# A hybrid encoder layer on one core: a third weight buffer, another step order in the linear attention, another split of the expert work over the engines, and expert products scattered by pair

## The reference

```
h = rmsnorm(x, norm_mix);  proj = h @ w_in
ya = (dilated window attention, 3 groups of 4 heads, merged by log-sum-exp) @ w_proj_a
o_f, o_b = gla_chunked(q, k, v, logg_f), flipped gla_chunked(...)      # 4 heads, chunks of 64
yb = (rmsnorm(o_f + o_b, gla_norm) * silu(og)) @ w_proj_b
x = x + (sigmoid(ma) * ya + sigmoid(mb) * yb) @ w_out
hm = rmsnorm(x, norm_moe)
# hier_moe: top-1 of 4 groups, top-2 of its 8 experts -> gate, zero elsewhere
for e in range(N_EXPERTS):                                             # 32 experts, inner width 256
    a = jax.nn.silu(h @ w_eg[e]) * (h @ w_eu[e])
    out = out + gate[:, e:e + 1] * (a @ w_ed[e])
x = x + out;  y = rmsnorm(x, norm_final)
```

## Time and profile before

| | us |
|---|---|
| median of three timed runs | 1405.68 |
| lowest and highest of them | 1402.28, 1409.32 |
| profiled execution, its own time | 1400.52 |
| span of its trace, first to last instruction | 1398.7 |
| expert stage in it, first gate product to last down product | 981.6 to 1359.5 |

### The profile page before, as it was taken

One profiled execution on the slowest core, in us unless ns is written; L12 is line 12 of the kernel. 1 busy time (PEld: TensorE's weight loads), 2 busy tenths in 40 slices (PEclk: granted clock), 3 DMA queues, 4 the chain that ended last, 5 costly groups with the idle time before them and its releaser, 6 DMA issues. The chain is left out here.

```text
span 1398.7 us, 19631 instructions
## 1 busy us (share of the span) xinstructions
PE 1206.4 (86%) x7864; PEld 1112.9 (80%) x7864; DVE 637.6 (46%) x1063; ACT 555.2 (40%) x905; POOL 443.8 (32%) x196
## 2 busy tenths in 40 slices
PE   5989999988989889999999989951888988889870
PEld 3989899787778678999999989951877877878860
DVE  5001312446534354522021041266477787887856
ACT  6223443435435253221122130241466566665622
POOL 2121120221020110221121151243466666666613
PEclk8999999998999999999999999975899999999985
DMA  6520101442130310212122123172599999999927
GB/s 245 177 61 30 31 10 41 119 126 57 35 91 1 91 40 10 77 38 68 61 68 68 60 95 107 40 255 98 177 320 327 304 340 343 349 338 315 337 108 270
DMA packets 158728, 200.39 MB, mean 143 GB/s; under 512 B 11625, under 2 KB 139773, under 8 KB 158654
## 3 DMA queue, kind: packets, MB, share of 16 engines
q1 hardware_dynamic: 151150, 183.41, 40.2%
q0 software_dynamic: 7504, 15.94, 3.3%
HBM read 179.32 MB, written 34.42 MB: 153 GB/s over the span
## 5 line engine op out<-in xcount | busy, mean ns | idle before, releaser
L841 POOL TENSOR_TENSOR w_lo<-raw,w_hi 128x2048 fp32r<-128x2048 f32 (+2 forms) x37 | 152.7, 4126 | 667.8 <-ACT w_hi L979 667.6
L1206 PE MATMUL bank<-hT_hi,w_hi 128*128 128x384 f32 (+1 forms) x656 | 225.6, 344 | 4.3 <-DVE hT_lo L1493 4.3
L1207 PE MATMUL bank<-hT_lo,w_hi 128*128 128x384 f32 (+1 forms) x656 | 222.1, 339 | 0.0
L1208 PE MATMUL bank<-hT_hi,w_lo 128*128 128x384 f32 (+1 forms) x656 | 222.1, 339 | 0.0
L900 POOL TENSOR_TENSOR lo_gate<-raw_gate,hi_gate 128x2048 fp32r<-128x2048 f32 x30 | 138.6, 4619 | 114.3 <-ACT hi_gate L968 114.2
L1753 DVE TENSOR_TENSOR lo_up<-raw_up,hi_up 128x2048 fp32r<-128x2048 f32 x31 | 112.7, 3634 | 51.6 <-ACT hi_up L968 51.6
L1206 PEld LDWEIGHTS bank<-hT_hi,w_hi 128*128 128x128 f32 (+1 forms) x656 | 124.3, 189 | 8.3 <-DVE hT_lo L1493 4.7
L1207 PEld LDWEIGHTS bank<-hT_lo,w_hi 128*128 128x128 f32 (+1 forms) x656 | 124.3, 190 | 0.9
L1208 PEld LDWEIGHTS bank<-hT_hi,w_lo 128*128 128x128 f32 (+1 forms) x656 | 124.0, 189 | 1.0
L1206 PE MATMUL bank<-w_hi,hT_hi 128*128 128x256 f32 x432 | 123.7, 286 | 0.0
L1208 PE MATMUL bank<-w_hi,hT_lo 128*128 128x256 f32 x432 | 123.0, 285 | 0.0
(11 more groups left out here) (289 smaller groups left out, 2908.3 us busy)
## 6 DMA issues: line engine op xcount, KB each, us to landing
raw_gate<-in_w_exp_gate SPq DMA_DIRECT2D x32, 1024.0 KB, 7.5
raw_up<-in_w_exp_up SPq DMA_DIRECT2D x32, 1024.0 KB, 10.5
raw_down<-in_w_exp_down SPq DMA_DIRECT2D x32, 1024.0 KB, 5.6
raw<-in_w_in SPq DMA_DIRECT2D x25, 1024.0 KB, 6.0
y_d<-m_y SPq DMA_DIRECT2D x32, 512.0 KB
y_d<-zeros SPq DMA_DIRECT2D x11, 512.0 KB, 7.3
raw<-in_w_in SPq DMA_DIRECT2D x8, 512.0 KB, 6.2
raw<-in_w_proj_b SPq DMA_DIRECT2D x4, 1024.0 KB, 5.0
```

Source lines behind the costliest of these rows:

```text
L841: pool.tensor_tensor(w_lo[:, g % 2, 0:kb, 0:n], raw[:, g % 2, 0:kb, 0:n], w_hi[:, g % 2, 0:kb, 0:n].bitcast(F32), ALU.subtract).then_inc(w ...
L1206: pe.matmul(out, l_hi, r_hi, start=j == 0, stop=False)
L1207: pe.matmul(out, l_hi, r_lo, start=False, stop=False)
L1208: ins = pe.matmul(out, l_lo, r_hi, start=False, stop=j == n - 1)
```

## The change

The source differs in five places.

1. `raw` and `w_lo` share three buffers, and the subtraction writes over its input. A group's load waits for the last product of the group three before it.
2. The list of steps: `comb` and all `mix` stand together; `decay` is cut into `soft`, `cumul` and `decay`; z and soft of head h+1 stand behind `kot` of head h, cumul in the midst of its states and outputs, and the six products of `vb` h+1 are spread among those. `vb` has two buffers. For the last head, `mb` 0 is spread in their place.
3. The experts: DVE takes over the subtraction for gate, ACT takes over `result`, PE runs gate e+1, aT e, xt e+2, up e+1, down e. POOL is left with index copies and indirect DMAs.
4. `y_d` has 1536 rows, one for each pair; POOL scatters the product rows there with an indirect DMA, in place of SP's stores. Rows of a slot that hold no pair have a number beyond the bound and move nothing. SP then reads `y_pair` in token order with six plain DMAs. The 11 stores of zeros go.
5. Gate, up and router weights are laid out `(p k) n`, eight consecutive rows of the matrix to a partition, with h2 permuted to match.

```diff
-        raw = at("raw", [P, 2, KD, GW], F32, 56)
+        raw = at("raw", [P, RAW, KD, GW], F32, 56)
+        w_lo = at("w_lo", [P, RAW, KD, GW], F32R, 56)
...
+        head = [S(kind="kot", h=h, q=q) for q in range(3)]
+        if h + 1 < GH:
+            head += gates(h + 1) + [S(kind="soft", h=h + 1)]
...
+        steps += head + interleave(body, proj("vb", h + 1) if h + 1 < GH else proj("mb", 0))
...
-            src = {"gate": A["w_exp_gate"][0].rearrange("e (k p) n -> p e k n", p=P),
+            src = {"gate": A["w_exp_gate"][0].rearrange("e (p k) n -> p e k n", p=P),
...
-                        sp.wait_ge(y_mm if x == "down" else gu_mm, e - WRING + 1 if r is not None else e)
+                        sp.wait_ge(weights_used[x], e - WRING + 1 if r is not None else e)
...
-                store(e, p)
...
+            pairs = y_d.rearrange("(i p j) n -> p i j n", p=P, j=2)
+            for i in range(NT):
+                sp.dma_start(y_pair[:, i, :, :], pairs[:, i, :, :]).then_inc(pair_in[i], 16)
...
+            def take_y(e, p):
+                pool.tensor_copy(y_idx[:, p:p + 1], pair_slot[:, bass.ds(e, 1)]).then_inc(y_copied, 1)
...
+            for e in range(2):
+                take_x(e, e)
+                gather(e, e)
 
             def tile(e, p, k, r, u):
-                if ahead(e, 3):
-                    pool.wait_ge(w_lo_done["gate"], e + 2)
-                    take_idx(e + 3, 1 - p, 2)
+
                 if ahead(e, 2):
-                    lo_gate(e + 2, p, later(r, u, 2)[0], e + 4 if ahead(e, 3) else NE)
-                if ahead(e, 3):
-                    gather(1 - p)
+                    pool.wait_ge(xt_mm, e + 1)
+                    take_x(e + 2, p)
+                    gather(e + 2, p)
+                pool.wait_ge(y_done, e + 1)
+                take_y(e, p)
+                scatter(e, p)
...
+            def result(e, p, k):
+                act.wait_ge(y_mm, e + 1)
+                if not (isinstance(k, int) and k == 0):
+                    act.wait_ge(y_out[p], k * 16)
+                for half in range(2):
+                    ins = act.activation(m_y[:, p, half * 512:(half + 1) * 512], psum[B_Y[half]][:, :], ACT.Copy)
+                ins.then_inc(y_done, 1)
...
             def tile(e, p, k, r, u):
                 if ahead(e, 1):
-                    gate_up(e + 1, 1 - p, later(r, u, 1)[0], 2)
+                    gate(e + 1, 1 - p, later(r, u, 1)[0], 2)
                 aT(e, p, 2)
                 if ahead(e, 2):
                     xt(e + 2, p, k + 1)
+                if ahead(e, 1):
+                    up(e + 1, 1 - p, later(r, u, 1)[0])
                 down(e, p, r)
```

More of the change, by code:

```diff
@@ L43 @@
 WRING = 3
+RAW = 3
 OVER = 11
@@ L189, in plan, with gates @@
         steps += interleave(r, other)
+    def gates(h):
+        return [S(kind="z", h=h, d=d, s=s) for d in range(2) for s in range(2)]
     v = proj("vb", 0)
[L192 to L205, removed]
+    steps += v[0:1] + [S(kind="comb")] + [S(kind="mix", i=i) for i in range(NT)] + v[1:NT]
@@ L207, in heavy @@
+    steps += gates(0) + [S(kind="oaT", i=i) for i in range(NT)] + v[NT:]
+    steps += [S(kind="soft", h=0), S(kind="cumul", h=0), S(kind="wg", h=1), S(kind="decay", h=0)]
+    steps += proj("qkb", 1)
     def heavy(h):
-        r = [S(kind="kot", h=h, q=q) for q in range(3)]
+        head = [S(kind="kot", h=h, q=q) for q in range(3)]
+        if h + 1 < GH:
+            head += gates(h + 1) + [S(kind="soft", h=h + 1)]
+        body = []
         for first, n in SEQS:
             nc_ = 2 * n
-            r += [S(kind="state", h=h, first=first, nc=nc_, t=t, d=d) for t in range(nc_ - 1) for d in range(2)]
+            body += [S(kind="state", h=h, first=first, nc=nc_, t=t, d=d) for t in range(nc_ - 1) for d in range(2)]
@@ L230, in plan @@
     for m in range(4):
-        for name in ("ma", "mb", "pa", "pb"):
+        for name in ("ma", "mb", "pa", "pb") if m else ("pa", "pb"):
             steps += proj(name, m)
@@ L945, in _ @@
[L945 to L949 removed]
+                pool.wait_ge(xt_mm, e)
+                take_x(e, 0)
+                gather(e, 0)
+                pool.wait_ge(w_hi_done["gate"], e + 1)
@@ L952, in _ @@
+                pool.tensor_tensor(m_lo["gate"][:, 0], m_raw["gate"][:, 0], m_hi["gate"][:, 0].bitcast(F32),
+                                   ALU.subtract).then_inc(w_lo_done["gate"], 1)
+                pool.wait_ge(y_done, e + 1)
+                take_y(e, 0)
+                scatter(e, 0)
+            beyond(pool, beyond_tile)
         @block.scalar
@@ L966, in hi_weights @@
                 if not (isinstance(e, int) and e < ring):
-                    act.wait_ge(y_mm if x == "down" else gu_mm, e + (1 - ring))
+                    act.wait_ge(weights_used[x], e + (1 - ring))
                 act.activation(m_hi[x][:, p], m_raw[x][:, r], ACT.Copy).then_inc(w_hi_done[x], 1)
@@ L1171, in tile @@
                     hi_weights("down", e + 1, 1 - p, 2, *later(r, u, 1))
+                if ahead(e, 1):
+                    silu(e + 1, 1 - p, 2)
+                if ahead(e, 3):
+                    hi_weights("gate", e + 3, 1 - p, 2, *later(r, u, 3))
+                result(e, p, k)
             first_tiles(act.Fori, tile)
@@ L1212, in _ @@
                 k = s.kind
-                if k in ("w", "norm", "natural", "comb", "mix", "decay", "gstat", "mixT", "norm2", "route", "place"):
+                if k in ("w", "norm", "natural", "comb", "mix", "wg", "soft", "cumul", "decay", "gstat", "mixT", "norm2", "route", "place"):
                     continue
```

231 lines of the change are left out of this document (104 added, 127 removed).

## The result

The changed kernel takes 1637.2 us (median of 4 runs, 1633.9 to 1638.7), the kernel before 1407.0: a ratio of 1.164, 95% interval 1.160 to 1.168. The forecast was 1605 us, with a range of 1490 to 1700. The profiled execution took 1636.1 us, with a span of 1634.4.

What follows compares the result with a forecast made beforehand. Transfers and the ring of three weight slots were taken to bound the expert stage. 1400.5 us plus 228 (experts, late gather) minus 20 (linear attention) minus 3 (end) gave 1605.5 us, range 1490 to 1700.

Steps and rivals of the forecast that it cites:

- Gather behind the product, PE idle at `xt`: Expert stage: POOL gathers rows only after product and scatter, so PE waits at xt about 8 us in 29 tiles.
- The tile, 19.8 us: Expert stage: chain from one product's end to the next takes 19.8 us, ends 15.3 and 24.6, in 29 tiles.
- the landing: Expert chain: gathered rows arrive 4.1 us after the gather's instruction ends, chosen between 3.2 and 5.3.
- POOL's steps: Expert chain: y_idx copy, gap and scatter 2.0 us, x_idx copy and gap 0.95, gather 2.9, added before the landing.
- The gather beside `lo_up`: Expert chain: the gather's instruction meets DVE's lo_up and takes 2.9 us in place of 1.01.
- The clock: Expert stage: PE's half-speed clock after idle time costs 1.7 us a tile; mean falls from 0.95 to about 0.8.
- The linear attention, -20: Linear attention: new step order removes most PE waits for kot, ptg and the merge; -20 us, ends 0 and -40.
- The end, -3: End of kernel: last copy to first sum falls from 13.6 to 10.7 us with scatter and plain load, -3 us.
- The rival "PE finds its rows": Expert stage: rows arrive in time, tile 10.3 us, stage 330, whole kernel 1330 us; chance 0.05.
- The relief by the split: Expert stage: fewer transfers and rebalanced engines would bring a tile from 11.8 to 10 or 10.5 us; costed at nothing.

Runs made afterwards that it cites:

- e1: Changed kernel with POOL's gather of expert rows issued a tile earlier, ahead of the wait for the product: 1346.5 us, ratio 0.959 to the kernel before.
- e7: Kernel before with only the late gather: POOL gathers rows behind lo_gate and a wait for the product, no scatter: 1591.7 us, ratio 1.135.
- e12: Changed kernel with the gather ahead of the scatter, still behind the wait for the same product: 1628.3 us, ratio 1.159 to the kernel before.
- e3: Changed kernel with lo_up moved behind lo_x on DVE, out of the gather's way: 1647.1 us, ratio 1.171 to the kernel before.
- e4: Changed kernel with SP's weight loads spread: gate and up issued apart from down, not in one burst: 1604.6 us, ratio 1.142 to the kernel before.
- e10: e9 plus the spread weight loads of e4: 1320.5 us, ratio 0.940 to the kernel before, the fastest of all.
- e8: Changed kernel with each next expert's gate product computed three times, twice in PE's idle time before xt: 1640.2 us, ratio 1.170 to the kernel before.
- e2: Kernel before with the change's front part alone (step order, three raw buffers, two of vb, place of st): 1393.6 us, ratio 0.990.
- e11: e10 with the weight and h2 layout of the kernel before (1 KB runs): 1341.9 us, ratio 0.956 to the kernel before.
- e5: e1 plus the spread weight loads of e4: 1357.2 us, ratio 0.969 to the kernel before.
- e6: Kernel before with the change's layout alone (gate, up and router weights, h2): 1404.6 us, ratio 1.000.
- e9: Changed kernel with the gather another step earlier than in e1, ahead of the scatter, once transposes free the buffer: 1340.6 us, ratio 0.955.

## Why the prediction was right, and where only its sum was

- **Gather behind the product, PE idle at `xt`.** Right, and shown both ways: e1 takes it out of the change (-291 us), e7 puts it alone into the kernel before (+189). The wait is 9.1 us in 29 tiles; I had said about 8 in 29. By e12 it is the wait for the product that costs, not the order of scatter and gather behind it.
- **The tile, 19.8 us.** Measured 20.50. By steps: the gather starts at 4.64 (4.3 forecast), lasts 2.45 (2.9), lands 5.11 behind its end (4.1); `xt`, `up` and down take 1.97 + 3.41 + 2.91 = 8.3 (8.5, with the clock). The mis-sized term is **the landing**: I chose 4.1 between 3.2 and 5.3 because the gather came in the last third of 9.3 us of weight traffic. 1.0 us in 29 tiles is 29 us, more than the 21 by which the stage missed (626.9 against 606). The whole missed by 30.6 us (1636.1 in the profiled execution, against 1605.5): these 21, 9.2 of the linear attention and 0.5 of the end.
- **More than a size was wrong in that step.** The sum adds POOL's steps to the landing. e12 and e3 show that they don't add: rows come with the end of the 3 MB that SP issues on the same product's end, and 1.0 us later where the scatter stands ahead of them. Most of the 2.0 us for y_idx and scatter and of the 2.9 us for the gather was hidden behind this traffic. Chain and traffic happened to be about equally long (with the traffic spread `xt` comes 1.5 us earlier, e4; with the chain cut by 3.4 us 0.5 earlier, e12). That the total came out near is partly luck: the sum would have failed for any kernel in which one of the two is much the longer, as it did for e12 (99 us expected, 9 measured).
- **The gather beside `lo_up`.** The gather takes 2.45 us beside `lo_up` and 1.04 without (e3), and in e12 the scatter, which then meets `lo_up`, takes 2.4 in place of 1.02: the 2.9 of the sum was right in kind. In the change, in each of 28 tiles, the gather ends 0.91 or 0.92 us behind `lo_up`, and the copy `y_idx` 0.04 or 0.05 us behind `lo_gate`. The Trainium skill, "SBUF — State Buffer", section "SBUF: two separate sides", says that a DVE operation with two SBUF inputs and a GpSimd operation that reads SBUF take one shared pair of ports by an exclusive lock, and that the one that starts first keeps the other out for its whole length. The copy agrees with this. The gather too reads its row numbers from SBUF, and it is held (2.45 against 1.04 us); which part of its work is held no run shows. Taking the meeting away gained nothing: e3's tile is 20.90.
- **The clock.** The stage's mean is 0.76 (0.8 forecast) and `xt` to the product's end takes 8.3 us, 1.6 more than in e10 at a clock of 0.99 (6.7): about as forecast (1.7). e8 shows that filling the idle time gives none of it back.
- **The linear attention, -20.** By the traces -10.8 up to the first gate product, by e2's runs -14 with an interval of 9 to 19 that leaves the 20 out: this term was too large as well. The single waits behaved (kot 2.6 us, in the last head alone; ptg 3.2; o_att 0.7), 20 us less together. Not all of it arrived, since new work waits beside them (2.8 us at `et`), and 14.5 us of gain at the first product of `out` are 12.0 at the router and 10.8 at the gate. The products of `out` themselves take 2.4 us longer (90.4 in place of 88.0, first to last); why, and where the rest went, I did not settle.
- **The end, -3.** Measured -2.5, but by other steps: that it came so near is luck. The sum at 1374.4 in the earlier trace rows, which I took for the first, is that of the second block of tokens; the first one starts at 1371.2. So it was 10.4 us from the last copy's end to the first sum, not 13.6, and it is 8.6 now, not 10.7, because the last scatter lands in 2.6 us, not in 4.2:

```profile
1597.93 0.60 ACT m_y L1149
...
1599.54 2.60 DMA y_d<-m_y,y_idx
1602.25 4.85 DMA y_pair<-y_d
1607.12 1.30 DVE x L1825
```

- **The rival "PE finds its rows"** was 1330 us with a tile of 10.3, from 337 GB/s. e1 gave 1346 and 10.55, e10 1320 and 9.66: it was priced within 17 us as a kernel, and its condition is not met by the change. **The relief by the split** is real (e1 is 59 us below the kernel before, layout and front part included) and was rightly cost at nothing, because the chain hid it.

## What to carry to other kernels

In an engine's queue a prefetch must not stand behind the wait for the item in work, as it does when its line follows the write-back: the place of one line can serialize transfers and products that ran beside each other. Here it had to be ahead by a whole item (e1); ahead of the write-back but behind the same wait gave 9 us of 291 (e12). When one event releases both a chain and a burst of transfers, the longer of the two was the better guide here, not the sum: look at what is issued at the same moment before sizing a landing. Spreading the transfers and lengthening their runs paid 20 and 21 us once the rows were early (e10, e11); with the rows less early the one cost 11 us (e5), and in the old order the other gave nothing (e6).

## What the runs showed of the hardware

- Weight traffic moved at 395 to 434 GB/s in windows of 2 us of the change with the engines full (windows above), in packets of 4 KB (down) and 8 KB (gate and up). So the 337 GB/s at 0.99 of the kernel before, with gate and up in packets of 1 KB, were not the most that the memory gives in such a stretch. Over the 280 us from 1000 to 1280 us no run moved more than 342 GB/s (e9).
- Gathered rows and scattered rows issued beside 3.15 MB of weights landed, in the mean, 0.1 to 1.2 us behind the last of these, whether their instruction had ended at 3.7 or at 7.1 us (the change, e12).
- A one-column integer copy on POOL took 0.2 us alone and 1.5 us in the mean where DVE's subtractions of 2.3 us met it (e3). It ended 0.04 or 0.05 us behind the subtraction each time.
- With 5.8 of 9.1 us of idle time filled, 3.4 us at half speed still followed the 3.0 us left (e8). The tile changed by 0.2 us, the stage's mean clock from 0.75 to 0.92.
